# Two reorderings at the end of an attention tile: next scores ahead of the last weighting, softplus ahead of output roundings and weight splits

## The chip, the cores and the metric

The kernel runs on one core of one Trainium2 chip. The metric is the device time of one execution in microseconds. Five engines work from instruction streams of their own: TensorE (PE in the profile; its weight loads are PEld), VectorE (DVE), ScalarE (ACT), GpSimd (POOL) and SyncE (SP), which here issues all DMAs. Semaphores are the only order between them.

## The reference, cut to what matters

One decoder layer over 512 positions of width 1024: a SwiGLU block, a token mixer with two groups of eight attention heads, a second SwiGLU block and a gated embedding, each with RMS norms. The change lies in the mixer alone. Its stick-breaking heads compute, with z the scaled scores and softplus for -log(1 - beta):

```python
log_1m_beta = jnp.where(causal, jax.nn.log_sigmoid(-z), 0.0)      # minus softplus(z)
tail = lax.cumsum(log_1m_beta, axis=3, reverse=True) - log_1m_beta
a = jnp.where(causal, jnp.exp(jax.nn.log_sigmoid(z) + tail), 0.0)
out = einsum('bhqk,bhkd->bhqd', a, v)
# forgetting heads: softmax(q k^T / 8 + F[t] - F[s]) v, causal
merged = concatenate([rms_norm(o_sb, sb_group_g), rms_norm(o_fx, fox_group_g)])
return merged @ w_out
```

## The kernel before, in words

All float32 products are made from a rounded high part and a low part: three matmuls for one product. ScalarE makes the high part ("hi", a copy) and VectorE the low part (the difference). Weights come by DMA into four raw slots; `ahead` (L509 on ScalarE, L925 on VectorE) splits a unit of weights that TensorE needs four units later, and SyncE loads the next raw unit when the low part is made (`w_lo`).

The mixer works through four tiles (`mixer_tile`); a tile is two stick-breaking and two forgetting heads, one of each kind for `hh` 0 and 1 (`hd` = 2 * tile + hh). Tiles 0 to 2 are one loop body (`more` is true): beside their attention they project the queries, keys and values of the next tile (`project`, 24 matmuls for each of three columns in each `hh`). Tile 3 (`more` false) is written out apart and has parts of the output projection in those places (`parts`). The order on each engine is written by hand, and a semaphore wait holds up everything behind it on its engine.

On TensorE the end of a tile (`hh` 1) was: `project(2)`; the weighting of the forgetting heads `weigh(1, pt_r)` (L1750), which needs the split transposed weights (`pt_lo`); then `first_scores` of the next tile (L1649, L1651), which needs the doubled keys (`k_doubled`, a DMA at L384) and the free banks (`a_exp`). The next tile begins with a projection in tiles 1 and 2, and in tile 3 with `first_logits` (L1702 to L1706) and then `parts(0)`. The first unit of `parts(0)` reads the stick-breaking outputs of tiles 0 to 2, and so waits:

```python
if r == 0:
    pe.wait_ge(hold_ready, 6 * TILES - 2)
    pe.wait_ge(o_out, 2 * TILES - 3)
```

`o_out` counts one for each `out_lo`, two in a tile, so the value 5 is `out_lo(0)` of tile 2. Then come the transposes of v (L1657), and then the cumulative sum over softplus (L1735, 20 matmuls, called the triangular sum below), which waits for `sp_lo`, the low part of the softplus. Behind it stands `logits(1)` (L1702), which waits for `p_exp`, the exponential of the next tile's first logits.

ScalarE and VectorE do, at the end of a tile, these pieces: `softplus` (ScalarE: Abs, Exp, Ln of three score banks, L671 to L675, then the high parts, L679; VectorE: the sum, L1106, and the low parts, L1112), `out_copy`/`out_sum` (L763, L1224: two halves of an output bank are added), `out_hi`/`out_lo` (L770, L1231: the output times its gain, split; with a square, L773, that VectorE adds up, L957), `unit(4)` and `unit(5)` (weight splits) and `project_out` (L1086: a projected column leaves its bank).

Of the kernel before, what the change touches and what calls it, by code (L numbers as in the profile page):

```python
# [131 lines left out]
def build(nc, t, out):  # L132
# [7 lines left out]
    with ExitStack() as ctx:  # L140
# [357 lines left out]
        def _(act):  # L498
# [154 lines left out]
            def qk_split(tile, kind):  # L653

                first = isinstance(tile, int) and tile == 0
                act.wait_ge(hold_ready, (2, 4)[kind] if first else 6 * tile + 3 * kind)
                q, k, cq = ((q_both, k_twice, 0), (qf_both, kf_twice, 3))[kind]
                for hh in range(2):
                    act.activation(q[hh][halves[hh], :], hold[halves[hh], cq, :], ACT.Copy).then_inc(qk_hi, 1)
                    act.activation(k[hh][halves[hh], :], hold[halves[hh], cq + 1, :], ACT.Copy).then_inc(qk_hi, 1)  # L660
# [2 lines left out]
                act.wait_ge(v_t, 2 * tile + kind + 1)  # L663
                act.activation(v_r[kind][:, :, :, 0, :], v_source(kind), ACT.Copy).then_inc(v_hi, 1)

            def softplus(hd):

                for b in range(3):
                    e = el[:, 512 * b:512 * b + Z_W[b]]
                    act.wait_ge(z_done, 3 * hd + b + 1)  # L670
                    act.activation(e, Z[b][:, 0:Z_W[b]], ACT.Abs).then_inc(absz, 1)  # L671
                    act.wait_ge(absz, 3 * hd + b + 1)
                    act.activation(e, e, ACT.Exp, scale=-1.0).then_inc(exp_z, 1)  # L673
                    act.wait_ge(exp_z, 3 * hd + b + 1)
                    act.activation(e, e, ACT.Ln, bias=1.0).then_inc(lnz, 1)  # L675
                for b in range(3):
                    c = slice(512 * b, 512 * b + Z_W[b])
                    act.wait_ge(sp_full, 3 * hd + b + 1)
                    act.activation(sp_r[0][:, c], spf[:, c], ACT.Copy).then_inc(sp_hi, 1)  # L679
# [32 lines left out]
            def mixer_tile(j, more):  # L712
                for hh in range(2):
                    hd = 2 * j + hh

                    def unit(x):
                        if more:
                            ahead(U_MIX + TILE_UNITS, j, TILE_UNITS, 6 * hh + x)
                        elif x % 2 == 0:
                            for r, b in zip(PART_AT[hh][x // 2], PART_BANKS[hh][x // 2]):  # L720
                                if r < EVICTED:
                                    act.wait_ge(w_used, U_OUT + r + 1)
                                    act.activation(xg[:, 0, PART_ROW[r], :], bank[b][:, :], ACT.Copy).then_inc(part_hi, 1)
                                ahead(U_OUT, 0, 0, r)

                    def softmax_exp(i, b):
                        lb, at, w = L_AT[b]
                        src = L_BANKS[lb % 2][:, at:at + w]
                        first = 512 * lb + at

                        act.wait_ge(neg_max, 4 * hd + (1, 3, 3, 4)[i])
                        act.activation(pr[:, first:first + w], src, ACT.Exp, bias=stat[:, 0, b:b + 1],
                                       accum_out=stat[:, 1, b:b + 1]).then_inc(p_exp, 1)
                    if hh == 0:
                        v_split(j, 0)
                        v_split(j, 1)
                        if not more:
                            unit(0)
                    for i, b in enumerate((3, 2, 0)):
                        softmax_exp(i, b)  # L740
                    if hh == 1 and more:
                        unit(0)
                        unit(1)
                    act.wait_ge(tri_done, hd + 1)
                    for b in range(3):
                        c = slice(512 * b, 512 * b + Z_W[b])
                        act.activation(el[:, c], Z[b][:, 0:Z_W[b]], ACT.Exp).then_inc(a_exp, 1)
                        act.wait_ge(a_exp, 3 * hd + b + 2)
                        act.activation(sp_r[0][:, c], el[:, c], ACT.Copy).then_inc(a_hi, 1)
                    softmax_exp(3, 1)  # L750
                    if hh == 0 and more:
                        unit(0)
                        unit(1)
                    if hh == 1 and not more:
                        unit(0)
                    unit(2)
                    unit(3)
                    if hh == 1 and more:
                        qk_split(j + 1, 0)

                    def out_copy(kind):
                        act.wait_ge(o_done, 2 * hd + kind + 2)
                        act.activation(o_sum[halves[hh], kind, :], O_BANK[halves[0], :], ACT.Copy).then_inc(o_half, 1)  # L763

                    def out_hi(kind, gain):
                        if hh == 0:
                            return
                        act.wait_ge(o_added, 2 * hd + kind + 2)
                        g = gains[:, ds(GAIN_AT[gain] + j, 1)]
                        act.activation(oT[0][:, ds(j + 4 * kind, 1), :], o_sum[:, kind, :].unsqueeze(1), ACT.Copy,  # L770
                                       scale=g).then_inc(o_hi, 1)
                        act.wait_ge(added, ADD_AT[N_SB] + 2 * j + kind)
                        act.activation(o_sq, o_sum[:, kind, :], ACT.Square).then_inc(squared, 1)  # L773
                    out_copy(0)
                    for b in range(3):
                        c = slice(512 * b, 512 * b + Z_W[b])
                        act.wait_ge(pt_done, 3 * hd + b + 1)
                        act.activation(pt_r[0][:, c], PT_BANKS[b][:, 0:Z_W[b]],
                                       ACT.Copy).then_inc(pt_hi, 1)
                    if hh == 0:  # L780
                        softplus(hd + 1)
                        unit(4)
                        unit(5)
                        out_copy(1)
                    else:
                        if more:
                            qk_split(j + 1, 1)
                        unit(4)
                        out_hi(0, "sb_group_g")
                        unit(5)  # L790
                        out_copy(1)
                        if more:
                            softplus(hd + 1)
                        out_hi(1, "fox_group_g")


# [124 lines left out]
        def _(dve):  # L921
# [235 lines left out]
            def mixer_tile(j, more):  # L1157
                for hh in range(2):
# [13 lines left out]
                    def project_out(g):  # L1172
                        if more:
                            dve.wait_ge(w_used, U_MIX + TILE_UNITS + 6 * hh + 2 * g + 2 + TILE_UNITS * j)
                            hold_tile_column(3 * hh + g, G_BANK[:, :])
# [46 lines left out]
                    def out_sum(kind):  # L1222
                        dve.wait_ge(o_half, 2 * hd + kind + 1)
                        dve.tensor_tensor(o_sum[halves[hh], kind, :], O_BANK[halves[1], :], o_sum[halves[hh], kind, :],  # L1224
                                          ADD).then_inc(o_added, 1)
# [15 lines left out]
                    if hh == 0:  # L1241
                        softplus(hd + 1, 0)
                        softplus(hd + 1, 1)
                        project_out(2)
                        softplus(hd + 1, 2)
                        softplus_lo(hd + 1)
                        unit(4)
                        unit(5)
                        out_sum(1)
                    else:  # L1250
                        if more:
                            qk_split(j + 1, 1)
                        unit(4)
                        project_out(2)
                        out_lo(0, "sb_group_g")
                        unit(5)
                        out_sum(1)
                        if more:
                            for b in range(3):
                                softplus(hd + 1, b)  # L1260
                            softplus_lo(hd + 1)
                        out_lo(1, "fox_group_g")


# [140 lines left out]
        def _(pe):  # L1405
# [254 lines left out]
            def mixer_tile(j, more):  # L1660
                for hh in range(2):
# [110 lines left out]
                        first_scores(j, 1)  # L1772
                    project(2)
                    parts(2)
                    pe.wait_ge(pt_lo, 3 * hd + 3)
                    pe.wait_ge(o_added, 2 * hd + 2)
                    weigh(1, pt_r)
                    if hh == 1 and more:
                        first_scores(j + 1, 0)

            pe.wait_ge(consts, 1)
            keep_busy(14, bank[0])
# [132 lines left out]
```

## Time and profile before

| | |
|---|---|
| median of three runs | 1090.88 us (1089.4 to 1091.18) |
| profiled execution | 1091.4 us, span from first to last instruction 1089.5 us |
| TensorE busy | 1072.7 us of the span, mean granted clock 0.997 |
| VectorE busy, ScalarE busy | 621.1 us, 515.6 us |
| the three middle joints between tiles | 470.6, 524.2 and 577.8 us from the span's start |

A start time in the profile is in us from the first instruction. In the rows of a timeline the first number is the start, the second the duration; a bracket at the end says how long the engine had been idle before, and what ended it. An engine can start its next instruction somewhat before the duration of the last one is over, so the step from one start to the next is often shorter than the duration.

### The profile page before, as it was taken

The numbers are of one execution on the slowest core, as the hardware profiler recorded it, in microseconds if no ns is written. First come the engines' busy times: TensorE is split into PE (matmuls) and PEld (weight loads), VectorE is DVE, ScalarE is ACT, GpSimd is POOL, SyncE is SP. The second block draws the span as 40 slices with busy tenths as digits, with TensorE's granted clock in tenths as the row PEclk, the third lists the DMA queues.
The fourth block names the chain that finished last, engine by engine and source line by source line (L and its number), as shares of the span: only waits on it lengthen the run. The fifth ranks groups of instructions, "written<-read, shape, count | busy, mean of one in ns | idle before, by whom it ended". The sixth has DMA issues, their size and how long they took to land.

```text
span 1089.5 us, 15337 instructions
## 1 busy us (share of the span) xinstructions
PE 1072.7 (98%) x5014; PEld 897.4 (82%) x5014; DVE 621.1 (57%) x1047; ACT 515.6 (47%) x940; POOL 9.2 (1%) x29
## 2 busy tenths in 40 slices
PE   9999999999999999999999999999999999999997
PEld 8888888888888878888888887888888888888786
DVE  4545444544222689696969889554445445333655
ACT  5533333333222458696969846433333334333646
POOL 1000000000020000000000000000000000000000
PEclk9999999999999999999999999999999999999999
DMA  5332333232333332323222122323332334444002
GB/s 175 109 97 85 109 96 98 83 112 97 98 95 98 80 88 59 79 68 84 64 72 61 55 83 78 99 85 109 97 97 83 110 111 135 154 135 144 1 20 78
DMA packets 102195, 100.23 MB, mean 92 GB/s; under 512 B 7600, under 2 KB 85744, under 8 KB 102160
## 3 DMA queue, kind: packets, MB, share of 16 engines
q1 hardware_dynamic: 102160, 99.77, 31.2%
q8 instruction: 21, 0.34, 0.1%
q14 instruction: 14, 0.11, 0.0%
HBM read 94.44 MB, written 2.10 MB: 89 GB/s over the span
## 4 chain that ended last, share of the span: by engine, by line
PE 88%; DVE 6%; ACT 4%; issue 2%; DVEq 0%; POOL 0%; ACTq 0%; POOLq 0%
PE bank L1408 27%; PE bank L1409 27%; PE bank L1410 27%; PE bank L1735 2%; PE bank L1750 1%; DVE w_r L925 1%; DVE scratch L1313 1%; PE bank L1430 1%; ACT scratch L673 0%; DVE big L1095 0%; DVE big L1112 0%; DVE big L1092 0%; ACT scratch L671 0%; DVE big L1239 0%; PE bank L1649 0%
## 5 line engine op out<-in xcount | busy, mean ns | idle before, releaser
L925 DVE TENSOR_TENSOR w_r<-w_raw,w_r 128x512 fp32r<-128x512 f32 x332 | 225.3, 690 | 374.1 <-ACT w_r L509 373.9
L509 ACT ACTIVATE w_r<-w_raw 128x512 fp32r<-128x512 f32 x332 | 204.5, 628 | 403.0 <-PE bank L1410 397.0
L1408 PE MATMUL bank<-xg,w_r 128*128 128x512 f32 x890 | 349.5, 393 | 0.3 <-DVE scratch L1086 0.3
L1410 PE MATMUL bank<-xg,w_r 128*128 128x512 f32 x890 | 346.5, 389 | 0.0
L1409 PE MATMUL bank<-xg,w_r 128*128 128x512 f32 x890 | 346.5, 389 | 0.0
L1408 PEld LDWEIGHTS bank<-xg,w_r 128*128 128x128 f32 x890 | 167.1, 188 | 36.3 <-issue 1.4
L1410 PEld LDWEIGHTS bank<-xg,w_r 128*128 128x128 f32 x890 | 167.0, 188 | 35.0
L1409 PEld LDWEIGHTS bank<-xg,w_r 128*128 128x128 f32 x890 | 167.1, 188 | 34.4 <-issue 0.7
L1408 PE MATMUL bank<-big,w_r 128*128 (+1 forms) x416 | 162.7, 391 | 0.0
L1410 PE MATMUL bank<-big,w_r 128*128 (+1 forms) x416 | 161.9, 389 | 0.0
L1409 PE MATMUL bank<-big,w_r 128*128 (+1 forms) x416 | 161.9, 389 | 0.0
L1410 PEld LDWEIGHTS bank<-big,w_r 128*128 128x128 f32 x416 | 78.1, 188 | 16.4
L1409 PEld LDWEIGHTS bank<-big,w_r 128*128 128x128 f32 x416 | 78.1, 188 | 16.2 <-issue 0.2
L1408 PEld LDWEIGHTS bank<-big,w_r 128*128 128x128 f32 x416 | 78.1, 188 | 16.1 <-issue 0.2
L573 ACT ACTIVATE big<-scratch 128x512 f32 (+1 forms) x44 | 27.2, 633 | 27.3 <-DVE scratch L1026 27.3
L569 ACT ACTIVATE scratch<-scratch 128x512 f32<-128x512 f32 x44 | 27.1, 634 | 27.3 <-DVE scratch L1019 27.2
L1408 PE MATMUL bank<-big,xg 128*128 128x512 f32 (+1 forms) x88 | 32.9, 374 | 1.0 <-ACT rms L530 1.0
L1030 DVE TENSOR_TENSOR big<-scratch,big 128x512 f32 (+1 forms) x44 | 29.1, 691 | 6.1 <-ACT big L573 5.6
L1410 PE MATMUL bank<-big,xg 128*128 128x512 f32 (+1 forms) x88 | 32.6, 370 | 0.0
L1409 PE MATMUL bank<-big,xg 128*128 128x512 f32 (+1 forms) x88 | 32.6, 370 | 0.0
L546 ACT ACTIVATE xg<-xT,gains 128x512 fp32r<-128x512 f32 (+1 forms) x27 | 18.3, 676 | 22.3 <-DVE xT L980 22.2
L1735 PE MATMUL bank<-big,const_r 128*128 128x128 f32 (+3 forms) x160 | 26.6, 326 | 2.1 <-DVE big L1112 2.1
(177 smaller groups left out, 988.5 us busy)
## 6 DMA issues: line engine op xcount, KB each, us to landing
w_raw<-in_ffn_w_gate SPq DMA_DIRECT2D x88, 256.0 KB, 2.8
w_raw<-in_ffn_w_up SPq DMA_DIRECT2D x88, 256.0 KB, 2.8
w_raw<-in_ffn_w_down SPq DMA_DIRECT2D x88, 256.0 KB, 2.7
w_raw<-in_w_in SPq DMA_DIRECT2D x36, 256.0 KB, 3.1
scratch<-in_w_ple_gate SPq DMA_DIRECT2D x16, 256.0 KB, 3.2
w_raw<-in_w_in SPq DMA_DIRECT2D x24, 128.0 KB, 2.3
big<-big SPq DMA_DIRECT2D x24, 128.0 KB, 2.3
scratch<-in_x SPq DMA_DIRECT2D x4, 512.0 KB, 6.9
```

Of the source, the lines that this page charges most:

```text
L509: act.activation(w_slot(0, slot, 0, 4 * P), w_raw[:, slot, :], ACT.Copy).then_inc(w_hi, 1)
L546: act.activation(xg[:, 0, k, c], xT[:, k, c], ACT.Copy, scale=gains[:, g + k:g + k + 1]).then_inc(xg_hi, 1)
L569: act.activation(gu[a], gu[a], ACT.Silu).then_inc(silu_done, 1)
L573: act.activation(H[0][:, ds(2 * s + a, 1), :], gu[2 + a].unsqueeze(1), ACT.Copy).then_inc(h_hi_s, 1)
L925: dve.tensor_tensor(w_slot(1, slot, 0, 4 * P), w_raw[:, slot, :], plain(w_slot(0, slot, 0, 4 * P)), SUB).then_inc(w_lo, 1)
L1030: dve.tensor_tensor(H[1][:, ds(2 * s + a, 1), :], gu[2 + a].unsqueeze(1), plain(H[0][:, ds(2 * s + a, 1), :]), SUB).then_inc(h_lo_s, 1)
L1313: dve.tensor_tensor(gu[2 * a + half][:, c], banks[2 * half + a][:, c], rms[:, half, c], MUL).then_inc(y_half, 1)
L1408: pe.matmul(dst, w_hi_ap, m_hi, start=start, stop=False, skip_group_check=True)
L1409: pe.matmul(dst, w_lo_ap, m_hi, start=False, stop=False, skip_group_check=True)
L1410: return pe.matmul(dst, w_hi_ap, m_lo, start=False, stop=stop, skip_group_check=True)
L1430: pe.matmul(dst[:, 0:P], ones[:, :], ones[:, :], start=True, stop=True)
L1735: last = pe.matmul(Z[b][:, off:off + jw], lhs, sp_r[part][:, 512 * jb + jat:512 * jb + jat + jw], start=False, stop=(jc == TB - 1 and part ...
```

## The change

TensorE: in `hh` 1 of tiles 0 to 2 `first_scores(j + 1, 0)` now stands ahead of the last `weigh(1, pt_r)`. ScalarE: the Abs, Exp and Ln of `softplus(hd + 1)`, then `out_copy(1)`, then its high parts now stand ahead of `unit(4)`, `out_hi(0)` and `unit(5)`. VectorE: `project_out(2)`, the softplus sums, `out_sum(1)` and the softplus low parts stand ahead of `unit(4)`, `out_lo(0)` and `unit(5)`. Nothing is added or removed; SyncE's order is unchanged.

```diff
--- before.py
+++ after.py
@@ -663,9 +663,9 @@
                 act.wait_ge(v_t, 2 * tile + kind + 1)
                 act.activation(v_r[kind][:, :, :, 0, :], v_source(kind), ACT.Copy).then_inc(v_hi, 1)
 
-            def softplus(hd):
-
-                for b in range(3):
+            def softplus(hd, exps=range(3), rounds=range(3)):
+
+                for b in exps:
                     e = el[:, 512 * b:512 * b + Z_W[b]]
                     act.wait_ge(z_done, 3 * hd + b + 1)
                     act.activation(e, Z[b][:, 0:Z_W[b]], ACT.Abs).then_inc(absz, 1)
@@ -673,7 +673,7 @@
                     act.activation(e, e, ACT.Exp, scale=-1.0).then_inc(exp_z, 1)
                     act.wait_ge(exp_z, 3 * hd + b + 1)
                     act.activation(e, e, ACT.Ln, bias=1.0).then_inc(lnz, 1)
-                for b in range(3):
+                for b in rounds:
                     c = slice(512 * b, 512 * b + Z_W[b])
                     act.wait_ge(sp_full, 3 * hd + b + 1)
                     act.activation(sp_r[0][:, c], spf[:, c], ACT.Copy).then_inc(sp_hi, 1)
@@ -785,12 +785,14 @@
                     else:
                         if more:
                             qk_split(j + 1, 1)
+                            softplus(hd + 1, rounds=())
+                            out_copy(1)
+                            softplus(hd + 1, exps=())
                         unit(4)
                         out_hi(0, "sb_group_g")
                         unit(5)
-                        out_copy(1)
-                        if more:
-                            softplus(hd + 1)
+                        if not more:
+                            out_copy(1)
                         out_hi(1, "fox_group_g")
 
 
@@ -1250,15 +1252,16 @@
                     else:
                         if more:
                             qk_split(j + 1, 1)
+                            project_out(2)
+                            for b in range(3):
+                                softplus(hd + 1, b)
+                            out_sum(1)
+                            softplus_lo(hd + 1)
                         unit(4)
-                        project_out(2)
                         out_lo(0, "sb_group_g")
                         unit(5)
-                        out_sum(1)
-                        if more:
-                            for b in range(3):
-                                softplus(hd + 1, b)
-                            softplus_lo(hd + 1)
+                        if not more:
+                            out_sum(1)
                         out_lo(1, "fox_group_g")
 
 
@@ -1772,11 +1775,11 @@
                         first_scores(j, 1)
                     project(2)
                     parts(2)
+                    if hh == 1 and more:
+                        first_scores(j + 1, 0)
                     pe.wait_ge(pt_lo, 3 * hd + 3)
                     pe.wait_ge(o_added, 2 * hd + 2)
                     weigh(1, pt_r)
-                    if hh == 1 and more:
-                        first_scores(j + 1, 0)
 
             pe.wait_ge(consts, 1)
             keep_busy(14, bank[0])
```

VectorE, at the end of the loop body, from the last low part of a key on: here is what stood there before (L925 is `unit(4)`, L1086 `project_out(2)`, L1231 `out_lo(0)`, whose result is what `o_out` counts).

```order
L924 REGISTER_ALU
L925 TENSOR_TENSOR w_r<-w_raw,w_r 128x512 [waits w_hi]
L1086 SCALAR_TENSOR_TENSOR scratch<-bank,rms 128x512 [waits w_used]
L1231 ISA [waits o_hi]
L1231 ISA
L1231 SCALAR_TENSOR_TENSOR big<-sq,gains,big 128x512
L955 REGISTER_ALU [waits acc_zero]
L956 REGISTER_ALU [waits squared]
L957 TENSOR_TENSOR acc<-acc,rms 128x512 [waits added]
```

Behind it came `unit(5)`, `out_sum(1)` and the softplus. In the same place the changed kernel has the following, from its second softplus sum on (its lines stand two further: L1108 is the sum, L1226 `out_sum(1)`, L1114 the low parts, L927 `unit(4)`, L1233 `out_lo(0)`).

```order
L1108 SCALAR_TENSOR_TENSOR scratch<-bank,scratch 128x512 [waits lnz]
L1107 REGISTER_ALU
L1108 SCALAR_TENSOR_TENSOR scratch<-bank,scratch 128x256 [waits lnz]
L1225 REGISTER_ALU
L1226 TENSOR_TENSOR sq<-bank,sq 64x512 [waits o_half]
L1114 TENSOR_TENSOR big<-scratch,big 128x512 [waits sp_hi] x2
L1114 TENSOR_TENSOR big<-scratch,big 128x256 [waits sp_hi]
L926 REGISTER_ALU
L927 TENSOR_TENSOR w_r<-w_raw,w_r 128x512 [waits w_hi]
L1233 ISA [waits o_hi]
L1233 ISA
L1233 SCALAR_TENSOR_TENSOR big<-sq,gains,big 128x512
```

So all of the softplus, with its waits for ScalarE's Ln (`lnz`) and high parts (`sp_hi`), now stands ahead of the instruction that `o_out` counts, and ahead of the weight split.

TensorE, the end of the loop body: before, the last matmuls of the weighting and then the waits of the next scores.

```order
L1750 MATMUL bank<-big 128x128 x2
L1641 ISA
L1642 ISA [waits k_doubled]
L1643 ISA [waits qk_lo]
L1649 MATMUL bank<-big 128x512 [waits a_exp]
```

In the changed kernel this is the end of the loop body and the start of tile 3, from the loop's branch to the first matmul of `parts(0)` (L1705 to L1709 are `first_logits`).

```order
L1797 REGISTER_ALU
L1797 COMPARE_AND_BRANCH
L1705 MATMUL bank<-big 128x512 [waits fx_doubled0,qk_lo,first_v]
L1707 MATMUL bank<-big 128x512
L1709 MATMUL bank<-const_r 128x128
L1705 MATMUL bank<-big 128x384
L1707 MATMUL bank<-big 128x384
L1709 MATMUL bank<-const_r 128x128
L1705 MATMUL bank<-big 128x128
L1707 MATMUL bank<-big 128x128
L1709 MATMUL bank<-const_r 128x128
L1411 MATMUL bank<-big,w_r 128x512 [waits o_out,hold_ready,w_lo]
```

The scores stand ahead of these rows now and the weighting last in the body. The rows of tile 3 are as before: the first matmul of `parts(0)` waits for `o_out`, and the transposes and the triangular sum stand behind it.

## Rows read from the trace of the kernel before

**Rows 1.** The page's first part: busy time of each engine, share, instructions.

```profile
PE 1072.7 (98%) x5014; PEld 897.4 (82%) x5014; DVE 621.1 (57%) x1047; ACT 515.6 (47%) x940; POOL 9.2 (1%) x29
```

**Rows 2.** Waits of TensorE from 395 to 660 us: total, times, longest.

```profile
PE bank L1735 <- DVE big L1112: 2.1, 1, 2.1
PE bank L1657 <- DVEq L1303: 2.0, 1, 2.0
PE bank L1750 <- DVE big L1239: 1.3, 1, 1.3
PE bank L1408 <- DVE scratch L1086: 0.3, 2, 0.2
```

**Rows 3.** Timeline of TensorE, joint from tile 2 to tile 3: start, duration, instruction.

```profile
577.77 1.37 PE L1750 MATMUL bank<-big 128*128 128x512 f32 x8
578.99 0.67 PE L1649 MATMUL bank<-big 128*128 128x512 f32 x2
579.50 0.22 PE L1651 MATMUL bank<-const_r 128*128 128x128 f32 x1
...
582.08 0.45 PE L1408 MATMUL bank<-big,w_r 128*128 128x512 f32 x1
...
584.20 1.04 PE L1657 MATMUL bank<-ident,scratch 128*128 128x128 f32 x8
587.34 4.49 PE L1735 MATMUL bank<-big,const_r 128*128 128x512 f32 x20 [2.11 <-DVE big L1112]
591.67 0.33 PE L1702 MATMUL bank<-big 128*128 128x256 f32 x1
```

**Rows 4.** Timeline of ScalarE in the same stretch.

```profile
576.63 0.61 ACT L660 ACTIVATE big<-scratch 64x512 fp32r<-64x512 f32 x1
577.27 0.63 ACT L509 ACTIVATE w_r<-w_raw 128x512 fp32r<-128x512 f32 x1
...
580.19 0.60 ACT L671 ACTIVATE scratch<-bank 128x512 f32<-128x512 f32 x1
...
585.01 1.44 ACT L679 ACTIVATE big<-scratch 128x512 fp32r<-128x512 f32 x3
586.36 0.71 ACT L770 ACTIVATE big<-sq,gains 128x512 f32 x1
```

**Rows 5.** Timeline of VectorE in the same stretch.

```profile
578.96 0.69 DVE L1095 TENSOR_TENSOR big<-scratch,big 64x512 fp32r<-64x512 f32 x1
579.68 0.69 DVE L925 TENSOR_TENSOR w_r<-w_raw,w_r 128x512 fp32r<-128x512 f32 x1
...
580.89 0.74 DVE L1231 SCALAR_TENSOR_TENSOR big<-sq,gains,big 128x512 f32 x1
...
585.65 1.63 DVE L1112 TENSOR_TENSOR big<-scratch,big 128x512 fp32r<-128x512 f32 x3
```

**Rows 6.** Timeline of SyncE: the key doubling for tile 3.

```profile
571.87 1.68 SPq L384 DMA_DIRECT2D big<-big  x2
```

**Rows 7.** All transfers of L384, the key doubling.

```profile
DMA to landing us min/median/max: 2.2/2.3/2.3
```

**Rows 8.** Timeline of TensorE, joint from tile 0 to tile 1.

```profile
470.58 1.37 PE L1750 MATMUL bank<-big 128*128 128x512 f32 x8
...
484.32 0.33 PE L1702 MATMUL bank<-big 128*128 128x256 f32 x1
```

**Rows 9.** Timeline of all engines early in tile 1.

```profile
481.46 0.69 DVE L1086 SCALAR_TENSOR_TENSOR scratch<-bank,rms 128x512 f32<-128x512 f32 x1
...
482.06 1.34 DVE L1179 TENSOR_REDUCE stat<-bank 128x1 f32<-128x512 f32 x3
482.78 0.69 ACT L732 ACTIVATE scratch<-bank,stat 128x512 f32<-128x512 f32 x1 [0.33 <-DVE stat L1179]
```

**Rows 10.** Busy time by stretch; the eighth field is the granted clock.

```profile
585.20:587.30 2.10, 0.04 (x1) 0.00 (x0) 1.99 (x4) 2.10 (x5) 0.00 (x0) 0.98 0.00 0
587.30:590.50 3.20, 3.16 (x11) 2.97 (x12) 3.13 (x6) 3.20 (x8) 0.00 (x0) 0.50 0.00 0
```

## The prediction

> **What bounds the kernel now.** I read the page first: TensorE is busy for 1072.7 us of a span of 1089.5 us [rows 1], so a reordering on the other engines can gain only what TensorE waits, and it costs wherever TensorE begins to wait. The waits of TensorE around the mixer are therefore the second view [rows 2]. Inside the tiles they are few: 2.1 us ahead of the triangular sum of tile 3 (L1735, for VectorE's L1112, the low part of the softplus), 2.0 us ahead of the first transposes, which lies before the change, 1.3 us ahead of the last weighting of tile 3 (L1750), and 0.3 us in two places for `project_out(2)` (L1086). At the two joints between loop tiles TensorE waits for nothing else than that 0.3 us: the change can gain only at the joint from tile 2 to tile 3. The third view is the timeline there, engine by engine [rows 3, 4, 5], and the fourth the granted clock around the wait [rows 10]: after the idle 2.11 us it stands at 0.50 (1.2 GHz, the lower of two levels) for 3.2 us, so that the sum takes 4.49 us. The wait thus costs 2.1 us and then half of 3.2, 1.6 us.
>
> I count time at a joint from t = 0, where the last projection's matmuls end and the weighting begins: 577.77 at tile 3 [rows 3], 470.58 at tile 1 [rows 8].
>
> **The swap on TensorE.** The scores move ahead by the step of the weighting, 578.99 - 577.77 = 1.22 us, and the weighting back by that of the scores, about 1.7. Both are the same matmuls, so by itself this costs nothing. The scores need the doubled keys: the two transfers are issued from 571.87 for 1.68 us and land 2.3 us later [rows 6, 7], by 575.9 at the latest, 1.9 us before t = 0. That cover suffices; without it each 0.1 us of lateness would be 0.1 us of TensorE. What is queued behind the scores is the weighting, and only `out_copy(1)` waits for it.
>
> **The softplus on ScalarE.** Before, ScalarE began it at 580.19, t = 2.42, after two weight splits, `out_hi(0)` and `out_copy(1)`. Now it is free when `qk_split` ends, at 577.24, and waits for the first score bank. That is done 579.50 + 0.22 - 578.99 = 0.73 us after the scores begin [rows 3]; with 0.1 for the handing over (an estimate, VectorE's end at 587.28 to TensorE's 587.34 is 0.06) ScalarE starts at t = 0.85. The nine activations took 585.01 - 580.19 = 4.82 us [rows 4], so they end at 5.67. `out_copy(1)` follows (0.6, the duration of such a copy being that of L671), the high parts start at 6.2 and step on for 1.35 (585.01 to 586.36), to 7.55. The weight split ends at about 8.2 and `out_hi(0)`, 0.71, at about 8.9.
>
> **The softplus on VectorE.** `qk_split` ends at 579.65, t = 1.88 [rows 5], `project_out(2)` at 2.5, before the next tile's projection wants its bank at 2.9: the 0.3 us of L1086 in rows 2 are gained. The sums keep up with ScalarE. `out_sum(1)` starts when `out_copy(1)` is done, about 6.35, and takes 0.7 (as the L1095 of its size, 64x512, in rows 5); then the low parts, 1.63 us, end at 8.7. Before they ended at 587.28, t = 9.5. So the softplus comes early by 0.8 us and not by the length of what it passed, because it has to wait for the scores and because `out_sum(1)` stays ahead of its last piece. Behind it now stand `unit(4)` (step 0.6) and `out_lo(0)` (0.74): the latter ends at t = 10.05, where before it ended at 581.63, t = 3.86.
>
> **The joint into tile 3.** `parts(0)` of tile 3 starts at 582.08, t = 4.31, and waits for exactly that `out_lo(0)`; before it was ready 0.45 us earlier. Now TensorE stands still until t = 10.1, 5.8 us. The transposes of v and the triangular sum are queued behind `parts(0)`, so nothing fills the hole. From 10.1 on: the parts 584.20 - 582.08 = 2.12, the transposes 1.04, and the triangular sum starts at 13.3, when its softplus has been ready for 4.6 us. Before it started at 587.34, t = 9.57. The loss is **3.7 us**. The old stall of 2.1 us is removed and counted in this difference. The clock: before, 1.6 us were lost after an idle of 2.1 us. The hole now is longer, and the first matmuls after it (parts, transposes) run at the lower clock in place of the sum. I take the same 1.6, which cancels. The bounds are: none, the new hole then costing 1.6 less than I sum, and a loss in proportion to the idle time, 1.6 x 5.8 / 2.1 = 4.4, which is 2.8 more.
>
> The Trainium skill (TensorE: Matmul & The Clock Gate, Part 1, on the clock gate) says that the array's default is the throttled state, that activity releases it, and that the cost of warming up again is a stretch of time and not a number of matmuls. By that rule a longer idle time buys no longer slow stretch, and the sum would stay as it is; by the proportional reading it would be 2.8 us higher. The trace has idle times of one length only and can't tell these apart.
>
> **The joints into tiles 1 and 2.** Here there is no `parts(0)`; VectorE is the question. After `out_lo(0)` it has the square's addition, `unit(5)`, `out_lo(1)` and another addition, four operations of about 0.6 to 0.7 in step, so it is free at t = 12.45. Before, it went on to `project_out(0)` at 481.46, t = 10.88 [rows 9]: it is late by 1.55 us, since it idles while ScalarE makes the softplus. What is late next is the first maximum (482.06, t = 11.48, now 13.05) and ScalarE's first exponential (482.78, 12.2, now 13.75; with its 0.69 us it ends at 14.45). TensorE asks for it at `logits(1)`, 484.32, t = 13.74 [rows 8]. It had 0.85 us to spare; now it waits **0.7 us**, in each of two joints. Such a hole is a third of the 2.1 us that lowered the clock [rows 3, 10], so I cost no clock for it; if it did, that would be up to half of 3.2, 1.6 us more at a joint. `project(1)` behind it needs the weights of `unit(4)` and `unit(5)` (t = 9.4 and 11.2) and the bank of `project_out(0)` (13.15): all there. The loads of the following weights wait for these splits in SyncE's queue and come some 7 us later than before; their first use is a tile's second stage, beyond t = 16, hidden. SyncE's other transfers stand ahead of them and are released as before.
>
> **The sum.** 3.7 + 2 x 0.7 - 0.3 = 4.8 us. The profiled execution of 1091.4 us (span 1089.5) becomes 1096.2, the median of 1090.88 becomes **1095.7**. One thing is left out: ScalarE does the transposes' copies later in tile 3 and may reach the exponentials 0.4 us behind TensorE's sum; the attention of tile 3 runs close to ScalarE and VectorE up to the 1.3 us wait, so it may add up to 0.4. I say 1095.8.
>
> **The rivals.**
> A. The forecast, held at `parts(0)` and at `logits(1)`: 1094.9 to 1096.8, chance 0.60.
> B. The clock takes more than before: it stays low in proportion to the hole. For it: nothing in this trace shows the clock after 5.8 us idle. Against it: after 2.1 us it came back while TensorE simply worked on, 3.2 us later [rows 10]. 1090.88 + 4.8 + 2.8 = 1098.5; chance 0.15.
> C. Only the hole in tile 3 opens; VectorE keeps its old distance in the loop. For it: the margin is missed by only 0.7 us, worked out over ten steps. 3.7 - 0.3 = 3.4, 1094.3; chance 0.11.
> D. Faster: `out_lo(0)` does not hold `parts(0)`. Then the triangular sum starts with its softplus 0.8 us earlier, what is left of the stall, 1.3 us, is taken to cost no clock (it is shorter than the 2.1 us that did), and the gain is 0.8 + 1.6 + 0.3 = 2.7: 1088.2. The point from which it decides: the sum starts as early as before only if `out_lo(0)` ends by t = 9.57 - 3.16 = 6.4, that is 3.6 us earlier than reckoned. ScalarE's nine activations alone run to 5.7. Chance 0.07.
> E. The change moves nothing that can be measured, the hole in tile 3 being just as long in all as the old stall with its slow clock (3.7 us): the new one would have to cost no clock, and the joints of the loop nothing, with another 1.8 us gained. 1090.9, chance 0.07.
>
> **How the numbers follow.** A measurement of this kernel tells from no change about 0.2%, 2.2 us. Slower by more: A, B, C, 0.86; within: 0.07; faster: D, 0.07. The range leaves out D and E, 0.14, and a little of B's upper end: from 1093.3 (C with 1 us less, the run to run spread) to 1098.8 (B). The likeliest case's own range is 1094.9 to 1096.8.
>
> **What would show it.** TensorE idle for 5 to 6 us ahead of the first matmul of `parts(0)` in tile 3, released by VectorE's `out_lo` (L1233), and no wait at L1738, the triangular sum; a lower clock right after. At the first `logits(1)` of tiles 1 and 2 (L1705) an idle 0.5 to 0.9 us, released by ScalarE's exponential, and no more wait for L1088. ScalarE's Abs at 0.8 to 0.9 us after the scores begin. The prediction is wrong if the parts start before t = 8, if the slow stretch is much longer than 3.2 us, or if the moved scores wait for the keys.

## The result, and the profile after

The changed kernel takes 1096.61 us (median of six runs, 1095.7 to 1097.96) against 1090.93 us of the kernel before: 5.7 us slower, ratio 1.0055, 95% interval 1.0042 to 1.0068. The profiled execution took 1096.53 us with a span of 1094.7 us, 5.2 us over that of before. TensorE is busy as long as before; what was added is waiting. One execution of e3 below (2784 us) and one of e8 (1807 us, at a mean clock of 0.556) went far out of line and are left out of the ratios; they move neither median by more than 0.2 us. First line of the page's first part:

```profile
PE 1072.5 (98%) x5014; PEld 896.8 (82%) x5014; DVE 621.6 (57%) x1047; ACT 515.3 (47%) x940; POOL 9.2 (1%) x29
```

The waits of TensorE from 395 to 660 us (total, times, longest) answer to [rows 2]:

```profile
PE bank L1411 <- DVE big L1233: 5.6, 1, 5.6
PE bank L1705 <- ACT scratch L732: 2.2, 3, 1.0
PE bank L1660 <- DVEq L1306: 2.0, 1, 2.0
PE bank L1753 <- DVE big L1241: 1.2, 1, 1.2
```

The waits for L1086 and at the triangular sum are gone, as the change meant them to be. In their place stand one of 5.6 us ahead of the first matmul of `parts(0)` in tile 3, released by `out_lo` (L1233), and two of 1.03 us and one of 0.16 at `logits(1)` (L1705). TensorE's timeline at the joint into tile 3 answers to [rows 3]; t = 0 is now 579.09, the start of the scores:

```profile
579.09 0.62 PE L1652 MATMUL bank<-big 128*128 128x512 f32 x2
...
580.75 1.45 PE L1753 MATMUL bank<-big 128*128 128x512 f32 x8
...
589.15 0.77 PE L1411 MATMUL bank<-big,w_r 128*128 128x512 f32 x1 [5.58 <-DVE big L1233]
...
593.10 1.04 PE L1660 MATMUL bank<-ident,scratch 128*128 128x128 f32 x8
593.90 2.97 PE L1738 MATMUL bank<-big,const_r 128*128 128x512 f32 x20
596.71 0.33 PE L1705 MATMUL bank<-big 128*128 128x256 f32 x1
```

`parts(0)` starts at t = 10.06; before it was 4.31. The triangular sum stands behind it and starts at 14.8 where it was 9.57. The reason stands on ScalarE, here from the first Abs (L671) to `out_hi(0)` (L770):

```profile
579.80 0.60 ACT L671 ACTIVATE scratch<-bank 128x512 f32<-128x512 f32 x1 [1.24 <-PE bank L1654]
...
584.73 0.59 ACT L763 ACTIVATE sq<-bank 64x512 f32<-64x512 f32 x1
585.34 1.46 ACT L679 ACTIVATE big<-scratch 128x512 fp32r<-128x512 f32 x3
586.71 0.61 ACT L509 ACTIVATE w_r<-w_raw 128x512 fp32r<-128x512 f32 x1
587.23 0.71 ACT L770 ACTIVATE big<-sq,gains 128x512 f32 x1
```

and on VectorE, from `project_out(2)` (L1088) to `out_lo(0)` (L1233):

```profile
581.00 0.69 DVE L1088 SCALAR_TENSOR_TENSOR scratch<-bank,rms 128x512 f32<-128x512 f32 x1
...
586.08 1.63 DVE L1114 TENSOR_TENSOR big<-scratch,big 128x512 fp32r<-128x512 f32 x3
587.62 0.69 DVE L927 TENSOR_TENSOR w_r<-w_raw,w_r 128x512 fp32r<-128x512 f32 x1
588.25 0.75 DVE L1233 SCALAR_TENSOR_TENSOR big<-sq,gains,big 128x512 f32 x1
```

ScalarE has been idle for 1.24 us when the first score bank comes, goes through nine activations, `out_copy(1)` (584.73) and the high parts (585.34), and only then reaches the weight split and `out_hi(0)`. VectorE ends its low parts at 587.71, splits the weights, and ends `out_lo(0)` at 589.00; TensorE goes on at 589.15. The granted clock (eighth field) at the hole, for two stretches of it and two after it:

```profile
583.50:585.70 2.20, 0.07 (x1) 0.00 (x0) 1.47 (x3) 2.09 (x6) 0.00 (x0) 1.00 0.20 61
585.70:589.10 3.40, 0.00 (x0) 0.00 (x0) 3.37 (x7) 3.40 (x8) 0.00 (x0) 0.58 0.00 0
589.10:592.50 3.40, 3.35 (x8) 2.70 (x9) 3.37 (x6) 1.12 (x2) 0.00 (x0) 0.50 0.42 116
594.00:597.00 3.00, 3.00 (x25) 2.92 (x24) 2.59 (x6) 3.00 (x9) 0.00 (x0) 1.00 0.00 0
```

It fell inside the hole and stayed at 0.50 for 3.4 us after it: the nine matmuls of `parts(0)` took 593.10 - 589.15 = 3.95 us, in place of 2.12 in [rows 3].

The joint into tile 1, to be laid beside [rows 8]: TensorE's scores and `logits(1)`,

```profile
470.07 0.61 PE L1652 MATMUL bank<-big 128*128 128x512 f32 x2
...
484.66 0.38 PE L1705 MATMUL bank<-big 128*128 128x256 f32 x1 [1.03 <-ACT scratch L732]
```

and the engines ahead of it, beside [rows 9] (L1088 is `project_out(0)`, L1181 the first maximum, L732 the exponential):

```profile
482.50 0.69 DVE L1088 SCALAR_TENSOR_TENSOR scratch<-bank,rms 128x512 f32<-128x512 f32 x1
483.11 1.34 DVE L1181 TENSOR_REDUCE stat<-bank 128x1 f32<-128x512 f32 x3
483.83 0.69 ACT L732 ACTIVATE scratch<-bank,stat 128x512 f32<-128x512 f32 x1 [1.59 <-DVE stat L1181]
```

With t = 0 at 470.07, `project_out(0)` starts at 12.43 (10.88 before), the maximum at 13.04, the exponential at 13.76, and `logits(1)` at 14.59 in place of 13.74.

### The profile page after: what moved, and what is told of

The parts are those of the page before. It is cut to its first block, busy times and chain, and to the rows that moved or that the text cites. A ratio compares the mean times of both kernels' runs of the same rounds, so it can differ in the third digit from the quotient of the medians.

```text
span 1094.7 us, 15337 instructions
## 1 busy us (share of the span) xinstructions
PE 1072.5 (98%) x5014; PEld 896.8 (82%) x5014; DVE 621.6 (57%) x1047; ACT 515.3 (47%) x940; POOL 9.2 (1%) x29
## 4 chain that ended last, share of the span: by engine, by line
PE 88%; ACT 5%; DVE 5%; issue 2%; DVEq 0%; ACTq 0%; POOL 0%; POOLq 0%
PE bank L1411 27%; PE bank L1412 27%; PE bank L1413 27%; PE bank L1738 1%; PE bank L1753 1%; DVE w_r L927 1%; DVE scratch L1316 1%; ACT scratch L673 1%; ACT scratch L671 1%; PE bank L1771 1%; PE bank L1433 1%; PE bank L1652 1%; ACT scratch L732 0%; DVE big L1114 0%; DVE acc L947 0%
## 5 line engine op out<-in xcount | busy, mean ns | idle before, releaser
L927 DVE TENSOR_TENSOR w_r<-w_raw,w_r 128x512 fp32r<-128x512 f32 x332 | 225.3, 690 | 374.1 <-ACT w_r L509 373.9
L1028 DVE TENSOR_TENSOR scratch<-scratch 128x512 f32<-128x512 f32 x44 | 28.3, 685 | 0.0
```

The lines of the kernel that those rows point to most:

```text
L927: dve.tensor_tensor(w_slot(1, slot, 0, 4 * P), w_raw[:, slot, :], plain(w_slot(0, slot, 0, 4 * P)), SUB).then_inc(w_lo, 1)
L1028: dve.tensor_tensor(gu[2 + a], gu[a], gu[2 + a], MUL).then_inc(h_f, 1)
```

## The experiments

All times are medians; a ratio is to the kernel before, in runs on the same chip (its medians there are 1090.72, 1090.83 and 1090.99 us). For each kernel I also measured its trace between fixed points of TensorE: the three joints, each from `logits(1)` in `hh` 1 of one tile to `logits(1)` in `hh` 0 of the next (starts of L1702, L1705 or its like), and the whole of tile 3, from `logits(1)` in `hh` 1 of tile 2 to the start of the last weighting of tile 3.

| kernel | us | joint 0 to 1 | joint 1 to 2 | joint 2 to 3 | tile 3 |
|---|---|---|---|---|---|
| before | 1090.93 | 27.41 | 27.41 | 27.56 | 56.18 |
| the change | 1096.61 | 28.26 | 28.26 | 31.29 | 60.04 |
| e1, scores only | 1094.36 | 28.03 | 28.04 | 29.76 | 58.78 |
| e2, softplus only | 1103.77 | 29.53 | 29.53 | 33.38 | 62.10 |
| e3, out 0 ahead | 1090.27 | 27.06 | 27.07 | 26.35 | 56.20 |
| e4, unit 4 ahead | 1095.79 | 27.75 | 27.75 | 31.40 | 60.14 |
| e5, the change, hole filled | 1095.34 | 28.26 | 28.27 | 29.46 | 58.22 |
| e6, before, idle times filled | 1088.97 | 27.42 | 27.47 | 26.17 | 55.97 |
| e7, e3 filled | 1089.31 | 27.06 | 27.07 | 26.35 | 57.41 |
| e8, e4 filled | 1093.15 | 27.76 | 27.76 | 28.94 | 57.75 |
| e9, e2 filled | 1101.14 | 29.54 | 29.53 | 30.74 | 59.52 |

**e1, TensorE's half alone.**

```diff
+                    if hh == 1 and more:
+                        first_scores(j + 1, 0)
                     pe.wait_ge(pt_lo, 3 * hd + 3)
                     pe.wait_ge(o_added, 2 * hd + 2)
                     weigh(1, pt_r)
-                    if hh == 1 and more:
-                        first_scores(j + 1, 0)
```

> TensorE's half of the change alone: the next tile's scores ahead of the last weighting, ScalarE and VectorE in their old order. With t = 0 at the end of the last projection as in the prediction. Theory (the softplus is tied to ScalarE's and VectorE's own queues, not to the scores): the weighting ends at t = 2.93 in place of 1.22, and out_copy(1), which stands ahead of the softplus on ScalarE and before began at 1.81, has to wait for it, about 1.15 us. Everything behind is 1.15 late: triangular sum of tile 3 at t = 10.7 (9.57 before), its idle time 3.3 in place of 2.1 us; at logits(1) of tiles 1 and 2 a new wait of about 0.5 us each. Sum +2.0: 1092.9. Rival (scores are what the softplus waits for): the softplus starts earlier by 1.2, 1089.7 or less.

Measured: 1094.36 us, ratio 1.0038 (1.0025 to 1.0051). The theory's sign and place hold. ScalarE's timeline at the joint into tile 3, `out_copy(1)` and the first Abs:

```profile
581.39 0.59 ACT L763 ACTIVATE sq<-bank 64x512 f32<-64x512 f32 x1 [1.37 <-PE bank L1750]
582.00 0.60 ACT L671 ACTIVATE scratch<-bank 128x512 f32<-128x512 f32 x1
```

and the triangular sum on TensorE:

```profile
589.15 5.38 PE L1735 MATMUL bank<-big,const_r 128*128 128x512 f32 x20 [3.42 <-DVE big L1112]
```

`out_copy(1)` waits 1.37 us for the weighting, the softplus starts at 582.00 though its scores were ready long before, and the sum starts after 3.42 us idle. The waits at `logits(1)` are 0.45 us (0.5 expected). The time is 1.5 us above the 1092.9 expected: the joints give 0.6, 0.6 and 2.2 us, 3.4 together, of which the longer slow stretch behind the 3.4 us idle is a part (the sum took 5.38 us, 4.49 in [rows 3]). The rival, that the softplus waits for its scores, is refuted: it gained nothing from them.

**e2, ScalarE's and VectorE's half alone.** The two engines as changed, and in the changed kernel:

```diff
-                    if hh == 1 and more:
-                        first_scores(j + 1, 0)
                     pe.wait_ge(pt_lo, 3 * hd + 3)
                     pe.wait_ge(o_added, 2 * hd + 2)
                     weigh(1, pt_r)
+                    if hh == 1 and more:
+                        first_scores(j + 1, 0)
```

> ScalarE's and VectorE's half alone: the softplus ahead of the roundings and splits, TensorE in its old order, so the first score bank is ready 1.2 us later than in the changed kernel. Theory (both engines stand idle for the scores and everything behind them shifts with the first bank): out_lo(0) at t = 11.3 in place of 10.06, the hole ahead of parts(0) in tile 3 6.8 us, the waits at logits(1) 2.2 us each in place of 1.03: 3 x 1.2 = 3.6 above the changed kernel, 1100.2. Rival (the order alone costs, not the wait for the scores): as the changed kernel, 1096.6.

Measured: 1103.77 us, ratio 1.0125 (1.0111 to 1.014): 7.2 us above the changed kernel, where 3.6 was expected. The waits are as reckoned, 2.32 us at each `logits(1)` and 6.86 at `parts(0)`:

```profile
594.70 0.76 PE L1411 MATMUL bank<-big,w_r 128*128 128x512 f32 x1 [6.86 <-DVE big L1233]
...
598.67 1.87 PE L1660 MATMUL bank<-ident,scratch 128*128 128x128 f32 x8
600.24 3.02 PE L1738 MATMUL bank<-big,const_r 128*128 128x512 f32 x20
```

But the transposes take 1.87 us (1.04 in [rows 3]), so the clock was still low 4 us after the hole. By stretch:

```profile
592.00:594.00 2.00, 0.00 (x0) 0.00 (x0) 2.00 (x5) 2.00 (x6) 0.00 (x0) 0.50 0.00 0
594.00:602.00 8.00, 7.30 (x27) 6.27 (x28) 5.84 (x11) 3.78 (x7) 0.00 (x0) 0.60 0.17 49
602.00:604.00 2.00, 2.00 (x17) 1.91 (x17) 1.93 (x6) 2.00 (x8) 0.00 (x0) 1.00 0.00 0
```

The third joint is 2.1 us longer than in the changed kernel and the other two 1.3 us each, which is 4.6 of the 7.2 us. Another 1.6 us lie inside tile 2 (27.83 us from joint to joint, 26.23 in the changed kernel): there the clock fell behind the wait of 2.32 us at `logits(1)`, and behind the same wait in tile 1 it did not. Most of what is left lies behind the mixer, where the clock fell at the row sums in e2's trace and not in the changed kernel's (0.7 us).

```profile
541.00:545.00 4.00, 3.12 (x10) 2.54 (x11) 3.89 (x13) 3.89 (x11) 0.00 (x0) 0.67 0.00 0
```

So either half alone is slower than no change, TensorE's by 3.6 us and the other by 13 us. The swap of the scores is worth 7 us once the softplus stands where it does. But the reverse doesn't hold: TensorE's half alone (1094.36 us) is 2.2 us faster than the whole change (1096.61 us), so moving the softplus costs even with the swap in place.

**e3, the hold taken away.** ScalarE's and VectorE's pieces for the first output move ahead of the softplus. ScalarE stands idle there for 1.24 us; VectorE's idle time of 1.12 us in the changed kernel lies between its first and its second softplus sum, so there the piece pushes the first sum back into it:

```diff
                             qk_split(j + 1, 1)
+                            out_hi(0, "sb_group_g")
                             softplus(hd + 1, rounds=())
...
                         unit(4)
-                        out_hi(0, "sb_group_g")
+                        if not more:
+                            out_hi(0, "sb_group_g")
...
                             project_out(2)
+                            out_lo(0, "sb_group_g")
                             for b in range(3):
                                 softplus(hd + 1, b)
...
                         unit(4)
-                        out_lo(0, "sb_group_g")
+                        if not more:
+                            out_lo(0, "sb_group_g")
```

> The changed kernel with out_hi(0) on ScalarE and out_lo(0) on VectorE moved ahead of the softplus, into the time in which both engines wait for the scores (1.24 and 1.12 us idle in the changed kernel's trace). Theory (the hold of parts(0) by out_lo(0) makes the hole of 5.6 us, VectorE's lateness makes the waits at logits(1)): no hole at parts(0); VectorE 1.3 earlier, so no wait at logits(1) of tiles 1 and 2 and 0.3 gained at the joints; in tile 3 the triangular sum starts at t = 8.7, 0.9 earlier than before, and logits(1) waits for the exponential at t = 12.6, so that about 0.8 of it is kept. 1090.9 - 0.3 - 0.8 = 1089.8 (1088.5 to 1090.6), faster still where the clock is not lowered. Rival (the swap of the scores or the split units carry the loss): nearer to 1096.

Measured: 1090.27 us, ratio 0.9999 (0.999 to 1.0008): 6.3 us below the changed kernel, and not to be told from before. The wait at `parts(0)` and those at `logits(1)` of tiles 1 and 2 are gone with this one move. In tile 3 four shorter ones stand in their place, 2.6 us together: at `logits(1)` (L1709), `parts(1)` (L1415), the transposes (L1664) and the triangular sum (L1742). Above them is the wait of the last weighting (L1757). The waits of TensorE in its trace:

```profile
PE bank L1757 <- DVE big L1243: 1.2, 1, 1.2
PE bank L1709 <- ACT scratch L732: 1.0, 1, 1.0
PE bank L1415 <- DVE big L1104: 0.6, 1, 0.6
PE bank L1664 <- DVE sq L1228: 0.5, 1, 0.5
PE bank L1742 <- DVE big L1116: 0.5, 1, 0.5
```

The joints into tiles 1 and 2 gain 0.35 us each, and the one into tile 3 gains 1.21. But tile 3 as a whole takes 56.20 us, where it took 56.18: its gain is given back behind the joint, first in a wait of 0.6 us at `parts(1)` (L1415) for a low part that VectorE makes, and in the end at the last weighting (L1757), which waits for VectorE as before. I had expected 0.8 of it to be kept.

**e4, one weight split ahead instead.**

```diff
                             qk_split(j + 1, 1)
+                            unit(4)
                             softplus(hd + 1, rounds=())
...
-                        unit(4)
+                        else:
+                            unit(4)
                         out_hi(0, "sb_group_g")
```

and on VectorE `unit(4)` between `project_out(2)` and the softplus sums.

> The changed kernel with unit(4), one weight split on ScalarE (0.53) and VectorE (0.6), moved ahead of the softplus instead. Theory (each operation taken off VectorE's chain behind the softplus brings out_lo(0) and the next maximum forward by its step): out_lo(0) 0.6 earlier, hole 5.0 us; waits at logits(1) 0.4 each: 3 x 0.6 = 1.8 below the changed kernel, 1094.8. Rival (the hold comes from ScalarE's queue or from the scores): unchanged 1096.6.

Measured: 1095.79 us, ratio 1.005 (1.0038 to 1.0063), 1 us above the expectation. The waits at `logits(1)` are 0.52 us and the hole 5.07 us, each shorter by the step of one operation; but in this trace the joint into tile 3 isn't shorter at all:

```profile
585.96 0.77 PE L1415 MATMUL bank<-big,w_r 128*128 128x512 f32 x1 [5.07 <-DVE big L1235]
...
589.94 1.66 PE L1664 MATMUL bank<-ident,scratch 128*128 128x128 f32 x8
591.35 2.96 PE L1742 MATMUL bank<-big,const_r 128*128 128x512 f32 x20
```

The parts took 3.98 us and the transposes another 1.41 up to the start of the sum. The run alone was inconclusive; e8 was made to decide it.

**e5, the hole filled.** In the changed kernel, ahead of `parts(0)`:

```diff
                     if not more:
                         first_logits()
+                        if hh == 0:
+                            pe.wait_ge(hold_ready, 6 * TILES - 2)
+                            keep_busy(20, bank[4])
```

> The changed kernel with 20 calls of the small product of ones (0.25 us each, into the projection's bank, which parts(0) overwrites) in the hole ahead of parts(0) of tile 3; the hole stays as long, but TensorE is not idle in it. Theory (the hole costs its length and then a stretch at the lower clock, 1.8 us in the changed kernel's trace): parts(0) starts at the same t = 10.06, its nine matmuls take 2.1 in place of 3.95 us, 1096.6 - 1.8 = 1094.8. Rival (the lower clock is without weight, the matmuls behind the hole being held by something else): 1096.6.

Measured: 1095.34 us, ratio 1.0039 (1.0025 to 1.0053). TensorE's timeline, the products of ones, the start of `parts(0)` and the transposes:

```profile
583.95 4.68 PE L1433 MATMUL bank<-ones 128*128 128x128 f32 x40
589.70 0.47 PE L1411 MATMUL bank<-big,w_r 128*128 128x512 f32 x1 [1.07 <-DVE big L1233]
...
591.83 1.04 PE L1660 MATMUL bank<-ident,scratch 128*128 128x128 f32 x8
```

`parts(0)` starts no earlier (t = 10.07) but takes 2.13 us; the joint is 1.83 us shorter, the median 1.3. So the hole costs its length and 1.8 us of clock.

**e6, the idle times of the kernel before filled.**

```diff
                 first_scores(0, 0)
                 pe.wait_ge(f4_ready, 1)
+                keep_busy(7, bank[3])
...
                         first_logits()
+                        if hh == 0:
+                            pe.wait_ge(hold_ready, 6 * TILES - 2)
+                            keep_busy(8, bank[4])
...
+            keep_busy(8, bank[1])
             sum_halves(N_MIX_POST, (bank[0], bank[3]))
```

> The kernel before with the same small products where TensorE would stand idle for about 2 us: 7 calls ahead of the loop (for the wait at the transposes of tile 0), 8 ahead of parts(0) of tile 3 (for the wait at the triangular sum), and 8 ahead of the row sums after the output projection. Nothing else is changed and each wait ends when it did. Theory (each idle time of about 2 us lowers the clock in some executions, for up to 1.7 us each): 1088.6 (1087.5 to 1089.5), the time of the runs of the kernel before whose mean clock was 1.0, with less spread. Rival (idle time costs its length alone): 1090.9.

Measured: 1088.97 us, ratio 0.9982 (0.9973 to 0.9991). TensorE's waits, to be laid beside [rows 2]:

```profile
PE bank L1754 <- DVE big L1239: 1.3, 1, 1.3
...
PE bank L1408 <- DVE big L1100: 0.5, 1, 0.5
PE bank L1444 <- DVE acc L950: 0.5, 1, 0.5
PE bank L1658 <- DVEq L1303: 0.5, 1, 0.5
...
PE bank L1739 <- DVE big L1112: 0.3, 1, 0.3
```

The three waits of 2 us are 0.3 to 0.5 now, since the engine spends the rest on products of ones. A wait of 0.5 us at `parts(1)` for VectorE (L1408) is new. The joint into tile 3 is 1.39 us shorter, and again tile 3 as a whole keeps only 0.21 of it. The larger part of the gain comes from tile 0, where `logits(1)` starts at 429.14 and before at 430.64. The third fill gains nothing against this trace of before, whose clock had stayed at 1.00 there. Of all versions only this one and e7 have an interval that lies below 1.

**e7, both together.** The diff of e3, and the first and third fill of e6.

> The version with out_hi(0) and out_lo(0) ahead of the softplus (e3), with the same products ahead of the loop and ahead of the row sums; tile 3 has no long idle time left in it. Theory: the joints gain 0.35 us each, the clock stays up, 1088.1 (1087.3 to 1089.0), a little below e6. Rival (e3's gain at the joints is given back to ScalarE's and VectorE's chain in tile 3 entirely): as e6 less 0.7 or no better.

Measured: 1089.31 us, ratio 0.9988 (0.9979 to 0.9997), not below e6. The time is as the rival has it (no better than e6): the joints into tiles 1 and 2 keep their 0.35 us each. Tile 3 takes 57.41 us in this trace, where the clock went down around 590 us, behind the waits of 1.0 us at `logits(1)` and 0.6 at `parts(1)` that this order brings. e3's trace has the same order and the same waits in tile 3, kept its clock, and took 56.20 us; so the longer tile is not the order's alone.

**e8, e4 with its hole filled** (18 products, as in e5).

> The version with unit(4) ahead of the softplus (e4) with 18 small products in its hole ahead of parts(0), 4.5 us. e4 came out at 1095.8 where 1094.8 was expected, though its trace has a hole of 5.07 us and waits of 0.52 us as reckoned. Theory (the rest is the clock: in e4's trace the parts, the transposes and a part of the sum run at the lower one): with TensorE busy in the hole the three steps of 0.6 us show in full against e5: 1095.34 - 1.7 = 1093.6. Rival (what unit(4) gives is taken back elsewhere in tile 3): 1095.3.

Measured: 1093.15 us, ratio 1.0021 (1.0012 to 1.0029), against e5 2.2 us less and 0.50, 0.51 and 0.52 us less at the three joints. The clock had hidden in e4's trace what the split gave. The joints make up 1.5 of the 2.2 us; the rest isn't placed by these traces.

**e9, e2 with its hole filled** (25 products).

> ScalarE's and VectorE's half alone (e2) with 25 small products in its hole, 6.2 us. e2 came out at 1103.8 where 1100.2 was expected. Theory (a hole of 6.9 us costs its length and some 3 us more by the clock): third joint 30.7 in place of 33.4 us, 1101.1; what is left above 1100 comes of the clock lowered by the two waits of 2.3 us at logits(1), which stay. Rival (the surplus is in ScalarE's and VectorE's chain): 1103.8.

Measured: 1101.14 us, ratio 1.0097 (1.0083 to 1.0112), as expected; the joint into tile 3 is 30.74 us (30.7 expected). Of the two waits of 2.33 us that stay at `logits(1)`, one was followed by the lower clock in this trace: tile 1 takes 27.88 us between its joints where it took 26.23, and tile 2 takes 26.24.

## Why the prediction was right, and where it was not

**The hold at `parts(0)`.** Forecast: `out_lo(0)` ends at t = 10.05, parts at 10.1, idle 5.8 us. Measured: 9.91, 10.06 and 5.58. Each step of ScalarE's and VectorE's chain was met within 0.15 us: ScalarE's start 0.71 (0.85 forecast), end of the low parts 8.62 (8.7), the softplus 0.8 to 0.9 us early. The joint cost 3.73 us (3.7). e3 moves only the piece that is waited for, and takes away 3.84 us of tile 3 and 1.2 at each of the other joints: this shows the cause.

**The clock at this joint.** I let the old 1.6 us and the new loss cancel; the new one is 1.8 us (3.95 against 2.12 us for the parts; 1.83 in e5), and the old one was 1.5 (the sum's 4.49 us against 2.97 after the change). That the joint still came out at 3.73 us is luck: these 0.3 us were made up by the transposes, which I counted with 1.04 us and which the sum followed after 0.80 (593.10 to 593.90). Proportional growth, rival B, would have been 4.4 and is out for this trace: the clock had already fallen in the hole, so only what lay behind it was paid. It is not a fixed price, though, and the trace of before could have shown that: it has idle times of 2.0, 2.1 and 2.28 us, not of one length only, and the clock fell behind the first two and not behind the longest. After 6.86 us idle, e2 paid 2.6 us (33.38 - 30.74 against e9), and e4 2.5 after 5.07 (31.40 - 28.94). By the Trainium skill (TensorE: Matmul & The Clock Gate, Part 1, on the clock gate) warming up costs a stretch of time that varies from run to run, because what watches the array runs freely. The traces agree as far as they go, with 1.8, 2.5 and 2.6 us in no order of the idle times; they are single traces of different kernels.

**The joints into tiles 1 and 2.** Forecast: a wait of 0.7 us in each, and 0.3 us gained together at L1086. Measured: waits of 1.03 us, and 0.85 us lost at each joint against 0.55. The step that failed is the subtraction of the 0.3: TensorE does start its projection earlier, but then stands at `logits(1)`, whose release comes from VectorE's and ScalarE's chain and is counted from the scores. Here a gain ahead of a later wait on the same engine was absorbed by that wait. The release itself came at 14.59, forecast 14.45. e4 and e8 (one operation less in the chain, 0.5 us less at each joint) show that this chain sets it. That a wait of this length costs no clock came true in this trace: the granted clock is 1.00 from 484 to 488 us.

**The sum.** 3.7 + 1.4 - 0.3 = 4.8 became 3.73 + 2 x 0.85 = 5.4, and 0.13 more to the end of tile 3, where up to 0.4 was left open. The measured 5.7 us lie by 0.1 beyond that; the stretches between the joints are 0.1 us longer. The profiled spans differ by 5.2 us only, because in the trace of the change tile 0 reached its `logits(1)` 0.47 us earlier (430.17, 430.64 before), ahead of everything that was changed.

**What the old stall was worth.** Here the text was wrong, without effect on the forecast. It put the wait of 2.1 us and the clock's 1.6 at the triangular sum down as a cost of 3.7 us, and rival D's gain of 2.7 us came for the most part from it. e3 and e6 shorten the joint into tile 3 by 1.21 and 1.39 us, and tile 3 as a whole by -0.02 and 0.21. The last weighting of tile 3 waits 1.2 to 1.3 us for VectorE in the traces of before, of the change, of e3 and of e6 alike: ScalarE's and VectorE's attention of this tile sets its end, with almost no slack on their side, so TensorE's earlier stall was in great part free. The hole of the change was not, since ScalarE and VectorE wait in it too.

## What to carry to other kernels

When a chain is moved ahead on an in-order engine, list what it is moved past and who waits for that: here `out_lo(0)`, whose result a far part of TensorE's program read, with the very piece that was to gain queued behind it. Work that must wait for another engine should be put behind the short pieces that are ready, not ahead of them: one short piece on each of the two engines, moved ahead of the softplus to use up an idle time of 1.1 to 1.2 us, took away 6 us. And a stall is worth only what the next wait on the same engine leaves of it.

## What the runs showed of the hardware

The time of one and the same kernel is uneven by about 2 us, and this goes with the clock. Of the 55 executions of the kernel before on the three chips of the experiments, the six with a mean clock of 1.000 took 1088.55 to 1088.98 us, those with 0.995 to 0.998 took 1090.3 to 1091.6. An idle time of 2 us lowered the clock in some executions and not in others. With the same wait of 2.0 us at the transposes of tile 0, the stretch behind it was this in the trace of before (granted clock in the eighth field)

```profile
426.40:430.40 4.00, 4.00 (x20) 3.90 (x19) 3.93 (x10) 2.51 (x8) 0.00 (x0) 0.57 0.47 131
```

and this in e3's:

```profile
424.00:428.00 4.00, 2.45 (x18) 2.36 (x19) 4.00 (x8) 2.86 (x7) 0.00 (x0) 1.00 0.24 55
428.00:432.00 4.00, 4.00 (x26) 3.59 (x25) 3.89 (x13) 3.88 (x11) 0.00 (x0) 1.00 0.26 76
```

It differs within one execution too: in the trace of before it fell behind the waits at L1657 (2.0 us) and L1735 (2.1 us), and ahead of the row sums (L1444, 2.28 us) it stayed at 1.00. Filling these three idle times with small products kept the clock up and was worth 1.9 us (0.18%).
